# A two-layer diffusion step on one core: another ring for late weight slices, another softmax order, another order in the first GLA pass

## The reference, cut to what matters

```python
def modulation(cond, w, b):
    m = jax.nn.silu(cond) @ w + b
    return [t[:, None, :] for t in jnp.split(m, MOD_CHUNKS, axis=-1)]

def sink_softmax(logits, sink):
    sb = jnp.broadcast_to(sink[:, :, None, None], logits.shape[:-1] + (1,))
    p = jax.nn.softmax(jnp.concatenate([logits, sb], axis=-1), axis=-1)
    return p[..., :-1]

def gla_chunk_scan(q, k, v, g, s0):
    def step(S, inp):
        bc = jnp.cumsum(gc, axis=2)
        o = jnp.einsum('bhcd,bhde->bhce', qc * jnp.exp(bc), S)
        decay = jnp.exp(jnp.where(causal, bc_i - bc_j, -jnp.inf))
        att = jnp.einsum('bhid,bhijd->bhij', qc, decay * kc[:, :, None, :, :])
        o = o + jnp.einsum('bhij,bhje->bhie', att, vc)
        S = (jnp.exp(bl)[..., None] * S + jnp.einsum('bhcd,bhce->bhde', kc * jnp.exp(bl - bc), vc))
```

## Time and profile before

| what | us |
|---|---|
| median of 3 runs | 3229.49 |
| lowest and highest of them | 3227.47, 3234.83 |
| the profiled execution, its own time | 3222.65 |
| its span | 3220.9 |
| mean granted clock of TensorE | 0.961 of full speed |

### The profile page before, as it was taken

The page is one execution under the profiler, slowest core; times in us unless marked ns, Lnnn a source line. Parts: engine busy times, 40 slices in busy tenths (PEclk is TensorE's granted clock), DMA queues, the critical chain, the costliest instruction groups (busy, mean ns, idle before and its releaser), DMA issues.

```text
span 3220.9 us, 39879 instructions
## 1 busy us (share of the span) xinstructions
PE 2972.4 (92%) x14994; PEld 2575.5 (80%) x14994; DVE 1636.6 (51%) x2527; ACT 1340.6 (42%) x2151; POOL 159.7 (5%) x260
## 2 busy tenths in 40 slices
PE   6888888888999999999999999777799999999998
PEld 3667676667899999999989877666679999999997
DVE  6444546664645454454442254766554545445444
ACT  6333333334544344344332366554444344334333
POOL 0000000000000000000000000873000000000000
PEclk8989989999999999999999999878899999999999
DMA  5444420005334443443331343001434444444443
GB/s 218 131 136 143 140 85 1 1 1 150 111 119 124 124 147 121 130 144 125 124 106 46 107 136 124 13 1 60 151 110 124 125 124 144 127 127 144 128 126 111
DMA packets 309592, 355.15 MB, mean 110 GB/s; under 512 B 20070, under 2 KB 242604, under 8 KB 308428
## 3 DMA queue, kind: packets, MB, share of 16 engines
q1 hardware_dynamic: 300560, 331.52, 32.9%
q10 hardware_dynamic: 6876, 13.87, 1.2%
q0 software_dynamic: 2016, 7.86, 0.7%
HBM read 337.88 MB, written 15.34 MB: 110 GB/s over the span
## 4 chain that ended last, share of the span: by engine, by line
PE 78%; DVE 9%; ACT 6%; issue 4%; DMA 3%; ACTq 0%; DVEq 0%; SPq 0%
PE ps L1897 35%; PE ps L1956 24%; PE ps L1746 7%; PE ps L2012 4%; PE ps L2099 2%; DMA mod_p<-mod_w 2%; PE ps L1687 2%; DVE smx L1386 1%; PE ps L1764 1%; DVE prob L1373 1%; DVE t_g L1409 1%; ACT junk_n L848 1%; DVE ps L1383 1%; PE ps L2116 1%; ACT mod_ph L726 0%
## 5 line engine op out<-in xcount | busy, mean ns | idle before, releaser
L1213 DVE TENSOR_TENSOR p_lo<-p_raw,p_hi 128x1024 fp32r<-128x1024 f32 x507 | 619.6, 1224 | 682.8 <-ACT p_hi L708 682.6
L708 ACT ACTIVATE p_hi<-p_raw 128x1024 fp32r<-128x1024 f32 x507 | 532.8, 1052 | 543.0 <-DMA p_raw<-mlp_w 398.7
L1956 PE MATMUL ps<-hm_hi,p_hi 128*128 128x384 f32 x1536 | 517.3, 337 | 4.8 <-DVE hm_lo L1233 4.0
L1956 PE MATMUL ps<-hm_hi,p_lo 128*128 128x384 f32 x1536 | 517.1, 337 | 0.0
L1956 PE MATMUL ps<-hm_lo,p_hi 128*128 128x384 f32 x1536 | 516.0, 336 | 0.0
L1897 PE MATMUL ps<-p_hi,hid_hi 128*128 128x512 f32 x1152 | 362.6, 396 | 1.9 <-DVE p_lo L1213 1.9
L1897 PE MATMUL ps<-p_lo,hid_hi 128*128 128x512 f32 x1152 | 357.3, 391 | 0.0
L1897 PE MATMUL ps<-p_hi,hid_lo 128*128 128x512 f32 x1152 | 356.5, 391 | 0.0
L893 ACT ACTIVATE relu<-ps 128x384 f32<-128x384 f32 x192 | 94.4, 492 | 547.9 <-PE ps L1956 547.9
L1447 DVE TENSOR_TENSOR sqr<-relu 128x384 f32<-128x384 f32 x192 | 107.2, 558 | 396.3 <-ACT relu L893 396.3
L1956 PEld LDWEIGHTS ps<-hm_hi,p_hi 128*128 128x128 f32 x1536 | 289.4, 188 | 14.1 <-DVE hm_lo L1233 4.5
(11 more groups left out here) (238 smaller groups left out, 4344.4 us busy)
## 6 DMA issues: line engine op xcount, KB each, us to landing
p_raw<-mlp_w SPq DMA_DIRECT2D x384, 512.0 KB, 3.8
mod_p<-mod_w SPq DMA_DIRECT2D x80, 512.0 KB, 4.1
p_raw<-gla_w_in SPq DMA_DIRECT2D x56, 512.0 KB, 3.6
p_raw<-gla_w_out SPq DMA_DIRECT2D x24, 512.0 KB, 3.4
mod_w<-mod_w SPq DMA_DIRECT2D x8, 1024.0 KB, 13.4
p_raw<-ab_w_in SPq DMA_DIRECT2D x14, 512.0 KB, 5.5
p_raw<-ab_w_out SPq DMA_DIRECT2D x12, 512.0 KB, 3.5
p_raw<-ab_w_out SPq DMA_DIRECT2D x24, 256.0 KB, 3.8
```

The lines of the kernel that those rows point to most:

```text
L708: nc.scalar.activation(p_hi[s][:, :, 0:width], p_raw[s][:, :, 0:width], ACT.Copy).then_inc(pan_hi, 1)
L1213: V.tensor_tensor(p_lo[s][:, :, 0:width], p_raw[s][:, :, 0:width], p_hi[s][:, :, 0:width].bitcast(F32), ALU.subtract).then_inc(pan_lo, 1)
L1956: mm = M.matmul(ps[:, b, 0:GN], w[s][:, c, :], x[:, c, :], start=(c == 0 and x is hi and w is p_hi), stop=(c == DC - 1 and w is p_lo))
```

## The change: what it does, and the diff

The late slices get 4 raw slots and 2 slots for high parts in the same memory; `mod_unit` gives two slices to most units, fewer to some convolution units, and the last slice follows unit 48 instead of 47; `late_rows` moves ahead of `unit_take` on ACT. In attention ACT runs the exponentials of step it first, and DVE the maximum of step it first; the normalising product moves from DVE to ACT, between the `prT` copy and `at_hi`. In the first GLA pass ACT computes the level-0 factor for Q ahead of the copy of the diagonal product; `att_out` is cut in two halves of two heads, after the products of levels 2 and 3; the transpose of the scaled K moves from level 5 to 6, and the taking of the output and the state step from level 4 to 5. PE's queue in attention is unchanged.

```diff
-MODS = 3
+MODS = 4
+MOD_HI = 2
...
+        mod_unit = []
+        for u in range(2, 49):
+            conv_u0 = u - CONV_UNIT
+            few = conv_u0 >= 0 and conv_u0 % 9 in (0, 4, 7)
+            mod_unit += [] if conv_u0 % 9 == 7 and few else [u] if few else [u, u]
+        mod_unit = mod_unit[:LATE]
...
-            return [k for k in range(LATE) if 2 + 46 * k // LATE == u]
+            return [k for k in range(LATE) if mod_unit[k] == u]
...
-                if k >= MODS:
-                    act.wait_ge(modp_used, FIRST_USED + k - MODS + 1)
-                nc.scalar.activation(mod_ph[k % MODS][:], mod_p[k % MODS][:], ACT.Copy).then_inc(mod_hi, 1)
+                if k >= MOD_HI:
+                    act.wait_ge(modp_used, FIRST_USED + k - MOD_HI + 1)
+                nc.scalar.activation(mod_ph[k % MOD_HI][:], mod_p[k % MODS][:], ACT.Copy).then_inc(mod_hi, 1)
...
+                for q in rows_after(u):
+                    late_rows(q)
                 unit_take(u)
                 for k in mods_after(u + 1):
                     late_hi(k)
-                for q in rows_after(u):
-                    late_rows(q)
...
             for it in range(len(steps) + 4):
+                if it < len(steps):
+                    b, j, u, tiles = steps[it]
+                    x = smx[:, it % 3, :]
+                    act.wait_ge(s_max, it + 1)
+                    if it >= 3:
+                        act.wait_ge(pt_ready, it - 2)
+                    nc.scalar.activation(prob[it % 3][:, 0:len(tiles) * P], s_bank(it)[:, 0:len(tiles) * P], ACT.Exp,
+                                         bias=x[:, 1:2], accum_out=x[:, 2:3])
...
                 if 3 <= it < len(steps) + 3:
...
+                if 1 <= it <= len(steps):
+                    b, j, u, tiles = steps[it - 1]
+                    pr = prob[(it - 1) % 3][:, 0:len(tiles) * P]
+                    act.wait_ge(s_sum, it)
+                    nc.scalar.activation(pr, pr, ACT.Copy, scale=smx[:, (it - 1) % 3, 5:6]).then_inc(s_norm, 1)
                 if it >= 4 and steps[it - 4][2] == 1:
...
-                if it < len(steps):
-                    b, j, u, tiles = steps[it]
-                    x = smx[:, it % 3, :]
-                    act.wait_ge(s_max, it + 1)
...
                 for level in range(NL):
                     if LEVELS[level] > 1:
                         exp_factor("S", tile, level)
+                    exp_factor("M", tile, level)
                     if level == 0:
...
-                    exp_factor("M", tile, level)
...
-                    if level == 4 and a:
+                    if level == 5 and a:
                         o_take(a - 1)
...
-                        att_out(a - 1)
-                    if level == 5 and tile != 1:
+                    if level in (2, 3) and a:
+                        att_out(a - 1, 2 * (level - 2), 2 * (level - 1))
+                    if level == 6 and tile != 1:
```

More of the change, by code:

```diff
@@ L108, in build @@
     mod_r4 = at("mod_r4", [4, 2 * D], F32, RS + 1024)
[L109 to L111 removed]
+    mod_p = [at(f"mod_p{i}", [P, 2, 512], F32, RW + (6 + i) * PANEL) for i in range(MODS)]
+    mod_pl = [at(f"mod_pl{i}", [P, 2, 512], F32R, RW + (6 + i) * PANEL) for i in range(MODS)]
+    mod_ph = [at(f"mod_ph{i}", [P, 2, 512], F32R, RW + (6 + MODS + i) * PANEL) for i in range(MOD_HI)]
     def acts(name, dt, r, chunks=DC):
@@ L815, in _ @@
             for it in range(len(steps) + 4):
+                if it < len(steps):
[6 more added lines that the diff above has]
+                                         bias=x[:, 1:2], accum_out=x[:, 2:3])
+                    head = j + 4 * u
+                    nc.scalar.activation(x[:, 3:4], sink[:, head:head + 1], ACT.Exp, bias=x[:, 1:2]).then_inc(s_exp, 1)
                 if 3 <= it < len(steps) + 3:
@@ L1351, in _ @@
             for it in range(len(steps) + 4):
+                if it < len(steps):
+                    b, j, u, tiles = steps[it]
+                    x = smx[:, it % 3, :]
+                    s = s_bank(it)
+                    dve.wait_ge(s_ready, it + 1)
+                    if it >= 3:
+                        dve.wait_ge(s_norm, it - 2)
+                    last = None
+                    for pos, (what, tile) in enumerate(tiles):
+                        if what == "own" and b and tile != b:
+                            cols = s[:, pos * P:(pos + 1) * P]
+                            last = V.tensor_tensor(cols, cols, band[:, 0 if tile < b else 1, :], ALU.add)
+                    if last is not None:
+                        own(last)
+                    own(V.tensor_reduce(x[:, 0:1], s[:, 0:len(tiles) * P], AX_X, ALU.max))
+                    head = j + 4 * u
+                    V.tensor_scalar(x[:, 1:2], x[:, 0:1], sink[:, head:head + 1], -1.0, ALU.max, ALU.mult).then_inc(s_max, 1)
+                if 1 <= it <= len(steps):
+                    x = smx[:, (it - 1) % 3, :]
+                    dve.wait_ge(s_exp, it)
+                    own(V.tensor_tensor(x[:, 4:5], x[:, 2:3], x[:, 3:4], ALU.add))
+                    V.reciprocal(x[:, 5:6], x[:, 4:5]).then_inc(s_sum, 1)
                 if 3 <= it < len(steps) + 3:
@@ L1365, in _ @@
                                     ALU.subtract).then_inc(ao_lo, 1)
[L1366 to L1388, removed]
             dve.wait_ge(mods_ready, 2)
@@ L1761, in late_mod @@
                 pe.wait_ge(mod_lo, FIRST_LO + k + 1)
-                for w in (mod_ph[k % MODS], mod_pl[k % MODS]):
+                for w in (mod_ph[k % MOD_HI], mod_pl[k % MODS]):
                     for a in range(2):
                         last = M.matmul(ps[0:4, 4 + q % 2, :], csr[:, 2 * (k % 4) + a, :], w[:, a, :],
-                                        start=(k % 4 == 0 and a == 0 and w is mod_ph[k % MODS]),
+                                        start=(k % 4 == 0 and a == 0 and w is mod_ph[k % MOD_HI]),
                                         stop=(k % 4 == 3 and a == 1 and w is mod_pl[k % MODS]))
@@ L2100, in gram, with att_out @@
                 last.then_inc(gram_ready, 1)
-            def att_out(a):
+            def att_out(a, h0, h1):
                 tile = TURNS[a]
[L2105 to L2114, removed]
+                if h0 == 0:
+                    pe.wait_ge(gram_taken, NL * (a + 1))
+                    if a:
+                        pe.wait_ge(ob_taken, a)
+                        pe.wait_ge(xt_ready, factor_at[("q1", tile, 0)] + 1)
+                    pe.wait_ge(khn_ready, min(a + 1, TILES - 1))
+                    if a == 1:
+                        pe.wait_ge(st_in, 16)
+                    if a >= 2:
+                        pe.wait_ge(st_ready, a)
+                for h in range(h0, h1):
                     o = psf[:, 3 * 512 + DV * h:3 * 512 + DV * (h + 1)]
@@ L2134, in _ @@
                         turn_k(kh, 3)
-            att_out(TILES - 1)
+            att_out(TILES - 1, 0, GH)
             def turn_k0(tile):
```

13 lines of the change are left out of this document (6 added, 7 removed).

## The result

| | before | after |
|---|---|---|
| median of 4 runs, us | 3229.52 | 3424.4 |
| lowest and highest | 3227.47, 3234.83 | 3422.49, 3425.93 |
| profiled execution, its own time | 3222.65 | 3424.69 |
| its span | 3220.9 | 3422.9 |

The changed kernel takes 1.060 times the time of before (95% interval 1.0582 to 1.0619): slower, as forecast (3460, range 3320 to 3525). Its profiled execution lies within 0.3 us of its median.

A forecast was written before the change was run, and what follows sets the result against it. PE was taken as busy nearly throughout, the change touching only three stretches where it is not: 3222.65 + 305 (attention) - 55 (input) - 20 (GLA) = 3453 us, forecast as 3460 us for the median, range 3320 to 3525.

The forecast's parts named there:

- the uncosted rest: All stretches outside input stage, attention and first GLA pass: no instruction changed, so costed at nothing.
- the last step to 3460: From the 3453 us sum to the median forecast, since the profiled execution before lies 6.8 us below its median.
- The chain in attention: Attention: transposes wait for the same iteration's softmax front; 6.44 us a step, plus 175 us at 2.4 GHz.
- The clock: Attention: PE's pauses let the clock fall; between 0 and 162 us more, four fifths taken, 130 us.
- rival 1: Low clock throughout attention, as in its first steps: 3491 us; chance 0.16.
- rival 2: High clock held in attention despite PE's pauses: 3330 us; chance 0.12.
- my strict reading: Attention: the skill's clock rule taken strictly, every pass starting slow, so all of the added price would be paid.
- The input stage: Input stage: the wait for the row of sums goes, with some slice waits and low clock; minus 55 us, bounds 35 and 69.
- the 42 and 3: Input stage: PE's 42.0 us of waits for the row of sums, and most of 3.4 us for a late slice, go.
- Rival 3: Input stage: the row's wait goes but PE then stands for slices, so no gain: 3515 us; chance 0.08.
- The GLA pass: First GLA pass: earlier level-0 factor and halved `att_out` save about 2.5 us in each of 8 turns; minus 20 us.
- Rival 4: Attention faster if PE can issue the transposes before the same iteration's exponentials are done: 45 us less, 3109 us; chance 0.04.

The follow-up runs named there:

- filler kernel: Changed kernel plus useless matmuls on PE between the scores and the transposes in attention, into an unused PSUM bank: 3303.59 us, ratio 1.0237 to the kernel before.
- the ring alone: Kernel before with only the new slots and slice table of the input stage, the row copy left behind the next slices: 3205.31 us, ratio 0.9907.
- the rows alone: Kernel before with only `late_rows` moved ahead of `unit_take`, three slots and the even table kept: 3172.44 us, ratio 0.9815.
- fifth run: Changed kernel with only ACT's attention copies moved ahead of the exponentials, DVE's order left as changed: 3348.08 us, ratio 1.0375 to the kernel before.
- the fastest kernel: Changed kernel with both engines' attention copies ahead of step it's exponentials and maximum, and the normalising product back on DVE: 3091.79 us, ratio 0.9582.

## Why the prediction was right, and where it was off

The sum was made on the profiled execution: 3453 forecast, 3424.7 measured, 28 us less. By terms: attention 14.2 less, input 11.7 less, GLA 7.8 less, the uncosted rest 5.7 more, together 28.0. So the total is not near by errors that cancel. Some 7 us more lie in the last step to 3460: I carried over that the profile of before lies 6.8 us below its median, and the changed kernel's does not.

- **The chain in attention (175 us for the order): right.** Fed with durations of before, it gave 6.44 us for a step at full clock, 13.3 for a pair, and some 3.2 us of wait in each step. The filler kernel shows a pair at full clock: its scores begin at 594.90, 601.37 and 608.41, steps of 6.47 and 7.04, 13.5 a pair. In the stage it is 169 us by the filler kernel, 166 by PE's idle time, and 206.7 us of waits in 69 steps where "about 200" was written. The piece that no row showed, the product on ACT, takes 0.72 us from start to start (714.94 to the `at_hi` at 715.66 on the changed kernel's timeline) where I took 0.62 between 0.48 and 0.79; so the product with V waits 0.52 for `at_lo` at the high clock, not 0.4. The Trainium skill ("ScalarE: Activation LUTs", section "What ACT_TABLE_LOAD costs") gives an instruction with one per-partition pointer operand about 0.28 us plus 0.833 ns an element, and an overlap of 0.093 between two: estimated from it for 640 elements 0.81 and 0.72, and the trace agrees (0.82 and 0.72).
- **The clock (130 of 162 us): right**, 122 by the filler kernel and 124 by PE's busy time. The granted clock was 0.59, between rival 1 (0.50 throughout) and rival 2 (held high), for the reason given: PE resumes slow after each pause and is quick only at the tail of a burst, in the timeline above of every second one. That four fifths of the work would be slow was a guess that no row gave; three quarters came (122 of 162), and that it came so near was luck. The row that I leaned on, 470 to 490 us at 0.50, is no row of pauses: PE was busy for 18.81 of its 20 us. The Trainium skill ("TensorE: Matmul & The Clock Gate", section "HAM oscillation — how this bites in real kernels") tells of a loop whose wait lets the clock fall, so that each pass starts slow. The trace agrees in that (T takes 1.30 us behind each pause); my strict reading, that the whole of the added price would be paid, is not borne out.
- **The input stage (-55): within its bounds, mis-sized in its clock term.** Waits went by 45.6 us, as the 42 and 3 said. But I let ten of the 24 us of low clock go, and 20.4 went: the clock was then 1.00. Over four kernels the clock rises as PE's idle time in the stage falls: 51.7 us and 0.94 before, 35.5 and 0.96 with the ring alone, 15.0 and 0.98 with the rows alone, 6.1 and 1.00 with both. So the low clock left with the waits. Rival 3, slices that PE waits for, did not come.
- **The GLA pass (-20): mis-sized.** I priced what PE and DVE waited for. The rows of before shown above have another 18.4 us in which ACT stood at the diagonal copy, and 34.6 us in which POOL, the busiest engine, stood for ACT; of these 3.4 and 8.3 us are left in the changed kernel. With the factor's line alone they are 5.7 and 10.7, so that line did most of it. And half of the 27.8 us is clock again (PE busy 13.8 less, idle 14.3 less). The halves of `att_out` were priced at under 1 us in a turn; the 4 us between the two stretches agree with it, but settle nothing.
- **Everything else at nothing**: 5.7 us more, 1.3 of it in the stage behind attention and 2.8 in the rest up to the GLA pass. Two executions of the same code differ by as much (the unchanged input stage ended at 462.3, 462.8, 467.5 and 468.2 in four profiles), so I claim no cause.
- **Rival 4, the faster side: its condition was wrong, its price right.** I wrote that it is "decided by one thing", and named as that thing ACT's `prT` copy alone ("if the `prT` copy were in time"). The fifth run mends exactly that and is still 3.7% slower than before. T waits for both engines' copies, and DVE's stands behind the maximum in the same way. My words on the change had "that copy now stands on ACT", and overlooked its twin on DVE, though the diff treats both alike. With both in time the price, 45 us for a step set by PE's 3.24 us, holds for the kernel with the product on DVE (273.2 - 229.7 = 43.5, and steps of 3.2 to 3.5 us); with the product on ACT, as the change has it, only 19.7 us come.

## What to carry to other kernels

When a queue's order is changed so that "the step that matters goes first", write down for each instruction of the other engines which iteration it belongs to, and follow the first wait of every engine back round the ring: if it comes back to the same iteration, nothing overlaps. Look for all twins of the late instruction, since the latest hides the rest: here mending one of the two gave 76 of 310 us, and mending the other nothing. And count a wait on PE twice where it drags the clock down: removing 46 us of waits gave 67 here, and adding 166 us cost 291.

## What the runs showed of the hardware that I had not expected

- Useless matmuls gained time: 2.42 us of them in each five-tile step, in a pause that was there anyway took the granted clock of the stage from 0.59 to 0.99 and the stage from 564.0 to 442.2 us. The right order was still worth far more (253.5).
- Shortening PE's pause from 3.23 to 2.39 us in each five-tile step moved the clock only from 0.59 to 0.64; with pauses of 0.5 to 0.9 us, in the filler kernel, it was 0.99.
- Once low, the clock can stay low while PE works with hardly a pause. Before, PE was busy for 2.48 of the 7 us from 463 to 470, and then for 18.81 of 20 us from 470 to 490 at a granted 0.50. In the fastest kernel it was busy for 1.99 of 5 us from 397 to 402, then for 9.56 and 10.00 of the next two 10 us, both granted 0.50. The mean was 1.00 again from 500 us in the one and from 432 us in the other. Pauses inside these 20 us can't be the reason; what else held the clock down no run here settles.
- The product by a per-partition factor on 128x640 floats in SBUF takes 0.82 us on ACT and 0.55 on DVE, 0.72 and 0.46 from start to start.
